# A hybrid GDN / MLA / mLSTM backbone step: the first level of the GDN inverse masked on VectorE, squares of o ahead of a take, last w_ada group ahead of the first gate products

## The reference, cut to what matters

```python
mod = jax.nn.silu(cond) @ p['w_ada'] + p['b_ada']
...
a = jnp.where(strict, jnp.einsum('bhncd,bhnsd->bhncs', kb, k) * decay, 0.0)
t = lax.linalg.triangular_solve(a + eye, jnp.broadcast_to(eye, a.shape), left_side=True, lower=True, unit_diagonal=True)
...
o = _rmsnorm(o_f + _flip(o_b), p['gdn_norm'])
```

## Time and profile before

| | |
|---|---|
| median of 3 runs | 3296.64 us (3293.19 to 3300.91) |
| profiled execution, whole | 3291.37 us |
| its span, first to last instruction | 3289.6 us |
| mean granted TensorE clock | 0.984 |
| GDN heads, layer 0 / layer 1 | about 230 to 730 us / 1850 to 2315 us |

### The profile page before, as it was taken

One profiled execution on the slowest core, in us unless ns is written; L12 is line 12 of the kernel. 1 busy time (PEld: TensorE's weight loads), 2 busy tenths in 40 slices (PEclk: granted clock), 3 DMA queues, 4 the chain that ended last, 5 costly groups with the idle time before them and its releaser, 6 DMA issues. The chain is left out here.

```text
span 3289.6 us, 64727 instructions
## 1 busy us (share of the span) xinstructions
PE 3092.9 (94%) x27490; PEld 2788.4 (85%) x27490; DVE 1223.9 (37%) x2462; ACT 826.0 (25%) x1698; POOL 2069.7 (63%) x2507
## 2 busy tenths in 40 slices
PE   6899999999999999999997999999999999999996
PEld 1488888889999997879986988889999999787996
DVE  1245545532322113442127447655333311345112
ACT  1323423411111213331005224433111122233000
POOL 3184434546666887446877735544777788653886
PEclk9999999999999999999998999999999999999998
DMA  8523433414444221113222322321222222111322
GB/s 321 198 91 109 139 106 104 138 63 132 127 135 135 77 71 65 35 45 104 74 76 102 112 71 92 101 93 60 78 84 86 88 72 73 54 39 37 115 77 112
DMA packets 122034, 319.93 MB, mean 97 GB/s; under 512 B 18256, under 2 KB 27600, under 8 KB 120592
## 3 DMA queue, kind: packets, MB, share of 16 engines
q1 hardware_dynamic: 91008, 263.38, 25.0%
q10 hardware_dynamic: 30736, 52.40, 4.6%
HBM read 302.65 MB, written 13.08 MB: 96 GB/s over the span
## 5 line engine op out<-in xcount | busy, mean ns | idle before, releaser
L489 POOL TENSOR_SCALAR w_hi<-raw 128x256 fp32r<-128x256 f32 x1232 | 1067.9, 892 | 1160.9 <-PE projection L589 673.7
L494 POOL TENSOR_TENSOR w_lo<-raw,w_hi 128x256 fp32r<-128x256 f32 x1232 | 952.0, 803 | 0.0
L587 PE MATMUL projection<-h_hi,w_hi 128*128 128x320 f32 x2304 | 763.5, 331 | 6.9 <-ACTq L1323 3.9
L589 PE MATMUL projection<-h_hi,w_lo 128*128 128x320 f32 x2304 | 715.0, 310 | 0.1
L588 PE MATMUL projection<-h_lo,w_hi 128*128 128x320 f32 x2304 | 714.1, 310 | 0.2 <-issue 0.2
L534 PE MATMUL projection<-h_hi,w_hi 128*128 128x320 f32 x1984 | 616.2, 311 | 20.7 <-POOLq L499 18.5
L535 PE MATMUL projection<-h_lo,w_hi 128*128 128x320 f32 x1984 | 613.7, 309 | 0.0
L536 PE MATMUL projection<-h_hi,w_lo 128*128 128x320 f32 x1984 | 613.5, 309 | 0.0
L587 PEld LDWEIGHTS projection<-h_hi,w_hi 128*128 128x128 f32 x2304 | 435.9, 189 | 47.6 <-issue 41.2
L588 PEld LDWEIGHTS projection<-h_lo,w_hi 128*128 128x128 f32 x2304 | 436.6, 189 | 0.5 <-issue 0.5
L589 PEld LDWEIGHTS projection<-h_hi,w_lo 128*128 128x128 f32 x2304 | 434.7, 189 | 0.7 <-issue 0.7
(11 more groups left out here) (399 smaller groups left out, 4306.5 us busy)
## 6 DMA issues: line engine op xcount, KB each, us to landing
raw<-in_w_stream SPq DMA_DIRECT2D x308, 512.0 KB, 3.3
fill<-in_w_fill SPq DMA_DIRECT2D x256, 256.0 KB, 2.7
work<-in_w_ada SPq DMA_DIRECT2D x64, 512.0 KB, 5.0
work<-rows ACTq DMA_DIRECT2D x32, 320.0 KB, 4.1
xo<-rows ACTq DMA_DIRECT2D x32, 320.0 KB, 5.0
xo<-in_x ACTq DMA_DIRECT2D x1, 5120.0 KB, 16.7
work<-in_x ACTq DMA_DIRECT2D x16, 320.0 KB, 5.2
x_kept<-xo ACTq DMA_DIRECT2D x4, 1280.0 KB, 4.5
```

Source lines behind the costliest of these rows:

```text
L489: nc.gpsimd.tensor_scalar(w_hi[:, s, cs, :], raw[:, s, cs, :], 1.0, None, ALU.mult).then_inc(split_part, 1)
L494: nc.gpsimd.tensor_tensor(w_lo[:, s, cs, :], raw[:, s, cs, :], w_hi[:, s, cs, :].bitcast(F32), ALU.subtract).then_inc(split_part, 1)
L587: mm(o, w_hi[:, half, c, :], h_hi[:, k, hs], start=(k == 0), stop=False)
L589: last = mm(o, w_lo[:, half, c, :], h_hi[:, k, hs], start=False, stop=(k == KT - 1))
```

## The change

- In levels 0 to 4 of the inverse, level 0 loses its four products. VectorE computes its outcome: for an identity the merged blocks are just the masked entries of KK, so four masks (one per group of 32 partitions) put them into the compact form BINV, `block_ident - BINV` gives BINV_T, and a transpose gives BINV. The mask for level 1 follows at once, per direction.
- ScalarE waits for VectorE's `level01` and no more for TensorE's `ld00` before it scales VB, EG and KBG.
- The cells are placed anew: 16 to 18 at the head's start, 9 to 10 before the levels, 4 to 3 behind them, and the two of level 0 fall away. The total stays 64.
- At a head's end ScalarE squares o first and takes tile 3 after it.
- At the start, group 3 of w_ada and both turns stand before the first eight gate cells.

```diff
@@ TensorE, start
                     group(2, range(4, KT))
+                    group(3, range(4))
+                    turned(2)
+                    group(3, range(4, KT))
+                    turned(3)
                     Q.wait("act", "rstd")
                     Q.leave()
                 gate_cells(range(KT // 2))
                 if l == 0:
-                    group(3, range(4))
-                    turned(2)
-                    group(3, range(4, KT))
-                    turned(3)
                     A.note()
@@ TensorE, GDN head
-                    ahead.cells(16)
+                    ahead.cells(18)
...
-                    ahead.cells(9)
+                    ahead.cells(10)
...
-                    for v in range(SQUARE + 1):
+                    for v in range(1, SQUARE + 1):
...
-                    ahead.cells(4)
+                    ahead.cells(3)
@@ ScalarE, GDN head
-                    B.wait("pe", "ld00")
+                    B.wait("dve", "level01")
...
-                    take(B, n0_, 3, xt(7))
                     B.wait("dve", "o whole")
                     B.did(A(wt(6), wt(4), ACT.Square), "o squared")
+                    take(B, n0_, 3, xt(7))
@@ VectorE, GDN head
+        def diagonal(ap, g):
+            return in_groups(ap)[g * BLOCK:(g + 1) * BLOCK, :, g, :]
+
+        def first_level(d, g):
+            return lvl[g * BLOCK:(g + 1) * BLOCK, d, 0, g * BLOCK:(g + 1) * BLOCK].unsqueeze(1).to_broadcast(
+                [BLOCK, TILES, BLOCK])
...
                     for d in range(2):
-                        B.did(tt(in_groups(LEVEL[d]), in_groups(KK[d]), own_group, ALU.mult), f"level{d}0")
-                    for v in range(SQUARE + 1):
+                        for g in range(ROW_GROUPS):
+                            last = tt(blocked(BINV[d])[g * BLOCK:(g + 1) * BLOCK, :, :], diagonal(KK[d], g),
+                                      first_level(d, g), ALU.mult)
+                            B.did(last, f"first{d}")
+                        B.wait("dve", f"first{d}")
+                        B.link(tt(blocked(BINV_T[d]), block_ident.unsqueeze(1).to_broadcast([P, TILES, BLOCK]),
+                                  blocked(BINV[d]), ALU.subtract))
+                        B.link(V.transpose(BINV[d], BINV_T[d]))
+                        B.link(tt(in_groups(LEVEL[d]), in_groups(KK[d]), own_group, ALU.mult), f"level{d}1")
+                    for v in range(1, SQUARE + 1):
```

More of the change, by code:

```diff
@@ L744, in _ @@
                     B.did(each_tile(wb, wt(1), wt(0)), "qk")
-                    ahead.cells(9)
+                    ahead.cells(10)
                     def block_of(ap):
                         return lambda t: ap[:, t * BLOCK:(t + 1) * BLOCK]
-                    for v in range(SQUARE + 1):
+                    for v in range(1, SQUARE + 1):
                         for d in range(2):
                             B.wait("dve", f"level{d}{v}")
-                            B.did(each_block((wa, wb)[d], LEVEL[d], block_of(BINV[d]) if v else lambda t: block_ident),
+                            B.did(each_block((wa, wb)[d], LEVEL[d], block_of(BINV[d])),
                                   f"ld{d}{v}")
@@ L757, in _ @@
                             B.wait("dve", f"prod{d}{v}")
-                            B.did(each_block((wa, wb)[d], PROD[d], block_of(BINV_T[d]) if v else lambda t: block_ident),
+                            B.did(each_block((wa, wb)[d], PROD[d], block_of(BINV_T[d])),
                                   f"dldT{d}{v}")
                         ahead.cells(1)
-                    ahead.cells(4)
+                    ahead.cells(3)
                     for v in range(SQUARE + 1, LEVELS):
@@ L1692, in _ @@
                             B.wait("pe", f"dldT{d}{v}")
-                            was = blocked(BINV_T[d]) if v else block_ident.unsqueeze(1).to_broadcast([P, TILES, BLOCK])
-                            B.link(tt(blocked(BINV_T[d]), was, blocked((wa, wb)[d][:, 0:BLOCKS_W]), ALU.subtract))
+                            B.link(tt(blocked(BINV_T[d]), blocked(BINV_T[d]), blocked((wa, wb)[d][:, 0:BLOCKS_W]), ALU.subtract))
                             if v < SQUARE:
```

## The result

| | before | after |
|---|---|---|
| median of 20 runs each, us | 3296.18 (3291.17 to 3302.21) | 3289.12 (3282.87 to 3294.93) |
| span of the profiled execution, us | 3289.6 | 3286.4 |
| mean granted TensorE clock | 0.984 | 0.981 |

The ratio of after to before is 0.9979, with a 95% interval of 0.9972 to 0.9985: 7.1 us faster, where 33 were forecast and the range ended at 3283. The direction was right, the size was not, and the time fell outside the range.

A forecast was written before the change was run, and what follows sets the result against it. TensorE, busy 94% of the span, was taken as the bound. Gains of 14.7 + 8 + 13.5 + 2 + 3.5 + 5 less 13.5 of new waits gave 33 us, from 3296.6 to about 3263, range 3243 to 3283.

The forecast's parts named there:

- The view of the bound: TensorE, busy for 94% of the span, bounds the kernel; an edit is worth what it takes from TensorE's work or gaps.
- parts 1 and 3: GDN heads on TensorE: 1x1 level's products removed, 14.7 us gained; squares of o before the take at head's end, 13.5 gained.
- part 1: TensorE's products of the 1x1 level, removed in 8 heads: 1.84 us per head, 14.7 us gained.
- Part 7: Start: group 3 of w_ada ahead of the first eight gate cells keeps the DMA queue fed, 5 us gained.
- Part 2: TensorE's unreleased gaps in the small products, put down to late instruction blocks: 1 us per head, 8 us gained.
- Part 5: Two more cells ahead of the sum of q fill layer 1's waits for its squares, 3.5 us gained; layer 0 neutral.
- Part 6: VectorE's added masks and level mask, 2.96 us per direction in layer 0, make TensorE wait for level 1: 13.5 us lost.
- Part 4: TensorE's clock: fewer 1.2 GHz stretches behind waits in the GDN heads, 2 us gained, between -4 and +7.
- VectorE's chain binds more: Rival: masks cost 0.45 us and level masks 1.0 in both layers, so waits are 28 us; 3278 us, chance 0.14.
- Blocks' pace: Rival: instruction arrival bounds the small products throughout, so removing them gains 20 us in gaps instead of 8; 3251, chance 0.17.
- Covers fail: Rival: the take delays the next cell like the square, and h_lo's chain and low clock bound the start; 3277, chance 0.08.
- The slower one: Rival: a 32-partition mask costs by its instruction; gain gone at 0.85 us each, 3313 at 1.1; slower or just even, chance 0.06.

The follow-up runs named there:

- e4_cells: The changed kernel with 16 instead of 18 cells ahead of the sum of q and 12 instead of 10 ahead of level 1: 3264.60 us, ratio 0.9904.
- e2_squares: The kernel before with only ScalarE's order at a GDN head's end changed, squares of o before the take: 3275.44 us, ratio 0.9942.
- e1_start: The kernel before with only the start changed, group 3 of w_ada and both turns ahead of the first eight gate cells: 3288.70 us, ratio 0.9979.
- e9_early: The changed kernel with two cells moved from ahead of the sum of q to the head's end, ten still ahead of level 1: 3272.06 us, ratio 0.9936.
- e10_cover: The changed kernel with 12 instead of 10 cells ahead of level 1, taken from the head's end, 18 still at its start: 3271.50 us, ratio 0.9932.
- e7_between: The changed kernel with 16 cells at the head's start, 11 ahead of the levels, 2 between level 1's two directions: 3248.68 us, ratio 0.9863.
- e6_more_masks: The changed kernel with eight more unread 32x160 masks per direction, four in one partition group, four in different ones: 3329.7 us in one execution.

## Why the prediction was wrong, point by point

**The view of the bound, parts 1 and 3: right.** 1280 matmuls are gone, and e4_cells, with as much time at 1.2 GHz as before, has 17.4 us less of TensorE's time without gaps (900.3 to 882.9) where part 1 had 14.7. The squares of o gave what their steps said and more: the wait of 15.2 us became 2.5, the heads of e2_squares are 14.2 us shorter, the kernel 19.3 (interval 15 to 23). The 0.54 us for the take was forecast as 0.5.

**Part 7, right.** 5 us forecast, 6.0 measured (interval 4 to 10). The wait for h_lo fell by 5.7 us in e1_start. The first GDN head begins at 227.8 to 231.1 us in the three traces with the old start and at 220.3 to 227.2 in the nine with the new one, 5.6 us earlier in the mean. A single pair of traces would not tell: e1_start's begins 10.8 us earlier than before's. The last w_ada product starts at 132.4 in after and at 140.5 before, sooner than the 136 expected:

```profile
L654 PE MATMUL wb<-work,cond x128: 592/592/617, 50.0 to 132.4; 128*32 128x512 f32 x128
```

```profile
L645 PE MATMUL wb<-work,cond x128: 592/592/1062, 50.3 to 140.5; 128*32 128x512 f32 x128
```

**Part 2, right in size over all kernels, half of it in this pair.** TensorE's unreleased gaps fell from 27.0 to 19.7 us at the small products, as forecast, but those in the cells grew from 1.3 to 4.3. The net is 4.3 us instead of 8. The sum scatters, however: over all heads it is 25.0 to 32.7 us in the four kernels with the old level (mean 29.1) and 17.1 to 25.3 in the eight with the new one (mean 20.8), 8.3 less. That late instruction blocks are the cause stays an inference from the even spacing of the gaps.

**Part 5, wrong where it says that the chain only moves.** The 3.5 us for the squares of q are gone. But "nothing is gained or lost" assumed that VectorE's chain only shifts. It shifted into GpSimd's pass and grew from 10.55 to 11.65 and 11.82 us. e9_early puts a price on it: with the two cells at the head's end the waits are 10.7 us less and the kernel 14 us faster (0.9979 to 0.9936).

**Part 6, the step that failed most.** It had 13.5 us of waits for the level mask, and 31.7 were measured. Its duration in quiet was right (2.96 us per direction, and 2.96 is what e9_early and e4_cells show for the first one in layer 0). Two things were not. First, the directions do not take 2.96 each, as GpSimd's passes fall on them. In five heads of after the first takes 3.6 and the second 3.8, in the last three of layer 1 the first takes 4.28 and the second 2.96. I had the proof in hand, the mask of 1.00 us in the earlier trace rows that I put down to GpSimd (it lies beside the lighter of the two passes, L489), and used it for one head only. Second, the chain ahead of the masks grew by 0.9 to 1.3 us, so TensorE arrived that much earlier against it. In the first head these are the whole sum: 0.6 forecast, 1.5 for masks and subtraction (level 1 ready 7.44 us behind the first mask instead of 5.96), 1.1 for the chain, 3.2. In layer 1 the first direction is late too, from the same two causes: TensorE stands there 1.9 us after the first mask (2002.37 against 2000.45), where the prediction had it 2.7 us after (2008.16 plus a cell and a burst, against 2006.63), and the mask is ready only after 4.28 us.

**Part 4, wrong in sign.** I set the stretches that the new waits bring about against those they replace, and took 2 us of gain. Of the 12 new waits in after 11 are of 2.2 to 3.3 us, as long as the 2.09 us ahead of the earlier trace rows or longer, against the eight of up to 2.1 us that went. The time at 1.2 GHz is 47.8 us instead of 20.5, at a loss of about 8 us. (The 20.5 are the four stretches that I counted and one at the start of each layer's first head, where after has one too.) A wait does not bring a stretch every time: behind the 3.18 us in layer 0's fourth head there is none. The price of half of a stretch was too high as well, as shown above. The error is one of multiplication: a wait that is mis-sized from 0.6 to 3.2 us brings its aftermath with it. The time at 1.2 GHz falls with the waits from after over e10_cover to e4_cells and e7_between, but it isn't a function of them: e9_early has 47.8 us at 21.0 us of waits.

**The rivals.** "VectorE's chain binds more" named the right mechanism, at 28 us of waits; it lay at 3278 because it charged the waits alone and not the clock behind them (8 us of loss in place of part 4's gain of 2 would have given 3288). The upper edge of the range, 3283, leaves out the clock in the same way: with part 4 at its own worst, -4 instead of +2, it would have been 3289. The lower edge is summed wrong: the blocks' pace and parts 4, 6 and 7 at their best give 3240 and not 3243. "Blocks' pace" would have taken 20 us off the unreleased gaps, and 8.3 went. "Covers fail" is refuted by e1_start and e2_squares. The slower one needed 0.85 us per mask; the longest in after are 0.79, and only two of a head's eight are of this kind.

## What to carry to other kernels

Price an instruction that you add to a second engine by the rows in which the third one works beside it, and look where that work lies after the edit: moving cells on the bounding engine also moves what they release. A new wait of 2 to 3 us on TensorE costs its own length and, often, the loss of a stretch of 3.4 us at 1.2 GHz behind it, 1.3 us in the small products here, so the range for a wait must hold both. When work is taken off the bounding engine and given to another, put the freed engine's filler behind what starts the other's chain (e9_early) and, where its second result is late, between its first result and its second (e7_between).

## What the runs showed of the hardware

A 32x160 fp32 mask on VectorE takes 0.32 us and follows its like after 0.23 us in the same partition group and 0.35 in another (e6_more_masks); beside GpSimd's two-tensor pass it takes 0.72 to 0.86 (81 masks in all traces), and a 128x640 instruction goes from 0.83 to 1.32 in after, but stays at 0.81 in L1681 and at 0.81 to 0.83 where one input is in PSUM. TensorE fell to 1.2 GHz at or behind single waits of 2 to 3 us in an otherwise dense stream, and stayed there for 3.4 or 6.8 us; 39.4 of the 47.8 us of this in after's heads lie over work. In the small products 3.4 us at 1.2 GHz cost 1.3 us. The gaps of TensorE that nothing released stand 256 or 512 instructions apart within a head, before and after alike.
